# A hybrid recurrent layer on one core: convolutions, level sums, opening and decode-state matmuls rearranged

## The reference, cut to what matters

```python
proj = jnp.einsum('bld,de->ble', rmsnorm(x, g_mix_pre), w_in)     # 2048 -> 7 rounds of 1024 columns, and 16
# A: HGRN2, 4 heads, state 128x128, chunked recurrence with decays
att = jnp.einsum('bhtd,bhsd,bhtsd->bhts', qi, ki, dec)
o = jnp.einsum('bhts,bhse->bhte', att, vi) + jnp.einsum('bhtd,bhde->bhte', qi * jnp.exp(b), S)
# B: gated DeltaNet, 8 heads: width-4 causal convolution + SiLU on q, k, v, then
sol = triangular_solve(eye + A, rhs)
u = sol[..., :DV] - jnp.einsum('bhtd,bhde->bhte', sol[..., DV:], S)
S_new = jnp.exp(b_last) * S + jnp.einsum('bhsd,bhse->bhde', ki * jnp.exp(b_last - b), u)
# C: RG-LRU, 512 channels, behind a width-4 causal convolution, times a GELU gate
x = x + rmsnorm(concat([oa, ob, oc]) @ w_out, g_mix_post)
x = x + rmsnorm((silu(h2 @ w_gate) * (h2 @ w_up)) @ w_down, g_ffn_post)     # h2 = rmsnorm(x, g_ffn_pre)
```

## Time and profile before

| | |
|---|---|
| median of three runs | 1403.34 us |
| profiled execution, its own time | 1404.58 us |
| its span, first to last instruction | 1402.9 us |
| PE busy | 1380.7 us, 98% |
| DVE busy | 839.1 us, 60% |
| ACT busy | 688.8 us, 49% |
| PE's granted clock, mean | 0.995 of full speed |

### The profile page before, as it was taken

One profiled execution on the slowest core, in us unless ns is written; L12 is line 12 of the kernel. 1 busy time (PEld: TensorE's weight loads), 2 busy tenths in 40 slices (PEclk: granted clock), 3 DMA queues, 4 the chain that ended last, 5 costly groups with the idle time before them and its releaser, 6 DMA issues.

```text
span 1402.9 us, 27846 instructions
## 1 busy us (share of the span) xinstructions
PE 1380.7 (98%) x11299; PEld 1356.7 (97%) x11299; DVE 839.1 (60%) x1137; ACT 688.8 (49%) x960; POOL 74.6 (5%) x154
## 2 busy tenths in 40 slices
PE   8999999999999899999999999999999999999998
PEld 6999999999999899999999999999999999999998
DVE  6778686866596957566655555555555544444443
ACT  6545656565565665555444444444444433343333
POOL 4010101010201000200000000000000000000000
PEclk9999999999999999999999999999999999999999
DMA  6453636363556455544655555555555555555552
GB/s 222 135 172 100 198 92 199 106 186 109 174 154 179 121 154 179 186 134 153 211 180 180 181 179 183 180 181 180 183 181 182 180 181 181 180 180 180 181 180 77
DMA packets 225253, 234.07 MB, mean 167 GB/s; under 512 B 10443, under 2 KB 220526, under 8 KB 224900
## 3 DMA queue, kind: packets, MB, share of 16 engines
q1 hardware_dynamic: 220500, 218.86, 50.0%
q0 software_dynamic: 4672, 14.04, 3.6%
HBM read 223.45 MB, written 9.65 MB: 166 GB/s over the span
## 4 chain that ended last, share of the span: by engine, by line
PE 89%; DVE 6%; ACT 2%; issue 2%; DMA 1%; SPq 0%; DVEq 0%; ACTq 0%
PE ps L626 26%; PE ps L627 26%; PE ps L628 26%; PE ps L805 1%; PE ps L913 1%; DVE w_lo L1602 1%; PE ps L821 1%; DVE conv L1748 1%; DVE TT L1836 1%; ACT w_hi L1147 1%; DVE rs L1849 1%; DMA xtok<-in_x_prompt_dram 1%; PE ps L755 1%; PE ps L745 1%; PE ps L1096 0%
## 5 line engine op out<-in xcount | busy, mean ns | idle before, releaser
L1602 DVE TENSOR_TENSOR w_lo<-raw,w_hi 128x1024 fp32r<-128x1024 f32 x408 | 500.1, 1227 | 438.0 <-ACT w_hi L1147 436.2
L1147 ACT ACTIVATE w_hi<-raw 128x1024 fp32r<-128x1024 f32 x408 | 432.1, 1061 | 572.3 <-PE ps L628 570.9
L626 PE MATMUL ps<-act_hi,w_hi 128*128 128x264 f32 x2296 | 666.2, 290 | 0.3 <-DVE xT L1662 0.3
L627 PE MATMUL ps<-act_lo,w_hi 128*128 128x264 f32 x2296 | 653.1, 284 | 0.0
L628 PE MATMUL ps<-act_hi,w_lo 128*128 128x264 f32 x2296 | 652.2, 284 | 0.0
L627 PEld LDWEIGHTS ps<-act_lo,w_hi 128*128 128x128 f32 x2296 | 434.5, 189 | 1.5
L626 PEld LDWEIGHTS ps<-act_hi,w_hi 128*128 128x128 f32 x2296 | 434.2, 189 | 1.8 <-DVE xT L1662 0.4
L628 PEld LDWEIGHTS ps<-act_hi,w_lo 128*128 128x128 f32 x2296 | 433.1, 189 | 0.0
L627 PE MATMUL ps<-hid_lo,w_hi 128*128 128x264 f32 x696 | 197.9, 284 | 0.0
L626 PE MATMUL ps<-hid_hi,w_hi 128*128 128x264 f32 x696 | 197.7, 284 | 0.0
L628 PE MATMUL ps<-hid_hi,w_lo 128*128 128x264 f32 x696 | 197.6, 284 | 0.0
(11 more groups left out here) (365 smaller groups left out, 1125.5 us busy)
## 6 DMA issues: line engine op xcount, KB each, us to landing
raw<-in_w_in_dram SPq DMA_DIRECT2D x112, 512.0 KB, 3.6
raw<-in_w_gate_dram SPq DMA_DIRECT2D x88, 512.0 KB, 3.5
raw<-in_w_up_dram SPq DMA_DIRECT2D x88, 512.0 KB, 3.5
raw<-in_w_down_dram SPq DMA_DIRECT2D x88, 512.0 KB, 3.5
raw<-in_w_out_dram SPq DMA_DIRECT2D x32, 512.0 KB, 3.6
out_dram<-Ss POOLq DMA_DIRECT2D x12, 512.0 KB, 5.0
Ss<-in_state_gdn_dram POOLq DMA_DIRECT2D x8, 512.0 KB, 6.4
xtok<-in_x_prompt_dram SPq DMA_DIRECT2D x2, 1024.0 KB, 6.0
```

Source lines behind the costliest of these rows:

```text
L626: pe.matmul(out, wh, x_hi[:, kk], start=(kk == begin), stop=False)
L627: pe.matmul(out, wh, x_lo[:, kk], start=False, stop=False)
L1147: return act.activation(out, in_, f, **kw)
L1602: tt(w_lo[:, slot], raw[:, slot], w_hi[:, slot].bitcast(F32), sub).then_inc(lo_done, 1)
```

## The change

Six things are changed; nothing is taken out of the computation.

1. DeltaNet rounds: DVE writes k and q of each state into a block of 32 columns (`kq_st`, zero elsewhere). PE uses this block as the stationary operand and the state as the moving one, sixteen matmuls in half-chunks 8 and 9, each group of 32 output partitions of bank 7 taking every fourth of them. ACT copies the bank out at position 5, PE turns it back with four transposes at half-chunk 11, and DVE reads every 32nd column.
2. HGRN2 rounds: the same for q (`q_st`) and the outputs, in one block at half-chunk 23, the copy by ACT at position 12 and the transposes at half-chunk 25.
3. The sum over eight levels becomes three adds of 512, 256 and 128 columns.
4. `ln_exp_tables` in `a_step` is no longer called.
5. The group-C convolutions move from DVE's positions 4 and 8 to 12 and 14, and from ACT's 6 and 10 to 13 and 15.
6. In the opening `turn_input(1)` becomes four `keep_busy` matmuls, and the three turns stand behind halves 0, 2 and 4.

```diff
@@ PE, b_step
-                if 7 <= hp <= 10:
-
-                    if hp == 7:
+                if hp in (8, 9):
+
+                    if hp == 8:
...
-                    for x in range(4 * hp - 28, 4 * hp - 24):
-                        last = pe.matmul(ps[:, 7, 2 * x:2 * x + 2], Ss[:, x, :],
-                                         nrm[:, :, x // 8, L + x % 8], start=True, stop=True)
-                    if hp == 10:
-                        last.then_inc(mx["ks"], 1)
+                        pe.wait_ge(mx["kp"], 2 * n + 2)
+                    for x in range(8 * hp - 64, 8 * hp - 56):
+                        c = 32 * (x % 4)
+                        last = pe.matmul(ps[c:c + 32, 7, P * (x // 4):P * (x // 4) + P], kq_st[:, x, :], Ss[:, x, :],
+                                         start=True, stop=True)
+                    if hp == 9:
+                        last.then_inc(mx["kw"], 1)
...
                 if hp == 11:
+                    pe.wait_ge(mx["kc"], n + 1)
+                    for g in range(4):
+                        last = pe.transpose(ps[:, 7, g * P:g * P + P], XM[:, g, :], ident)
+                    last.then_inc(mx["ks"], 1)
@@ PE, a_step
-                if 24 <= hp <= 26:
...
+                if hp == 23:
+                    pe.wait_ge(mx["sn"], 4 * n + 4)
+                    pe.wait_ge(a_["qp"], 2 * k + 2)
+                    for x in range(16):
+                        c = 32 * (x % 4)
+                        last = pe.matmul(ps[c:c + 32, 7, P * (x // 4):P * (x // 4) + P], q_st[:, x, :], Ss[:, x, :],
+                                         start=True, stop=True)
+                    last.then_inc(a_["vw"], 1)
+                if hp == 25:
+                    pe.wait_ge(a_["vc"], k + 1)
+                    for g in range(4):
+                        last = pe.transpose(ps[:, 7, g * P:g * P + P], QK[:, g, :], ident)
+                    last.then_inc(a_["vs"], 1)
@@ PE, opening
-                if hp in (0, 2):
-                    turn_input(2 + hp // 2)
+                if hp in (0, 2, 4):
+                    turn_input(1 + hp // 2)
...
-            turn_input(1)
+            keep_busy(4, 0, 2)
@@ ACT
+                if pos == 5:
+                    act.wait_ge(mx["kw"], n + 1)
+                    A(XM, quad(7)).then_inc(mx["kc"], 1)
...
-                    ln_exp_tables()
...
                 if pos == 12:
+                    act.wait_ge(a_["vw"], k + 1)
+                    A(QK[:, :, :], quad(7)).then_inc(a_["vc"], 1)
...
-                    if kind == "c" and pos in (6, 10):
-                        free_qkv(r, q - 1)
-                        silu_conv(12 + q - 1, q - 1, ACT.Copy)
                     mixer(pos)
+                    if kind == "c" and pos in (13, 15):
+                        i = (pos - 13) // 2
+                        free_qkv(r, i)
+                        silu_conv(12 + i, i, ACT.Copy)
@@ DVE
                 if pos == 0:
...
+                    dve.memset(u[:, :, :], 0.0).then_inc(mx["kp"], 1)
...
                 if pos == 3:
+                    dve.wait_ge(mx["kp"], 2 * n + 1)
+                    dve.tensor_copy(kq_st[:, :, 0:2].rearrange("p (j b) m -> p j b m", j=2),
+                                    nrm[:, :, :, L:T].rearrange("p m j b -> p j b m")).then_inc(mx["kp"], 1)
...
+                if pos == 11:
+                    dve.memset(q_st[:, :, :], 0.0).then_inc(a_["qp"], 1)
+                    dve.wait_ge(a_["qp"], 2 * k + 1)
+                    dve.tensor_copy(q_st[:, :, 0], q_s).then_inc(a_["qp"], 1)
...
-                    dve.tensor_reduce(attT[:, x, :], prod.rearrange("p l t -> p t l"), AX.X, ALU.add)\
-                        .then_inc(a_["rd"], 1)
+                    tt(prod[:, 0:4], prod[:, 0:4], prod[:, 4:8], add).then_inc(a_["rs"], 1)
+                    dve.wait_ge(a_["rs"], 2 * c + 1)
+                    tt(prod[:, 0:2], prod[:, 0:2], prod[:, 2:4], add).then_inc(a_["rs"], 1)
+                    dve.wait_ge(a_["rs"], 2 * c + 2)
+                    tt(attT[:, x, :], prod[:, 0], prod[:, 1], add).then_inc(a_["rd"], 1)
...
-                    if kind == "c" and pos in (4, 8):
-                        chained[0] = CV * (q - 1)
-                        convolve(12 + q - 1, (q - 1) % 2, 12 * CV, params[:, C_BIAS + 2 * (q - 1):C_BIAS + 2 * q])
                     mixer(pos)
+                    if kind == "c" and pos in (12, 14):
+                        i = (pos - 12) // 2
+                        chained[0] = CV * i
+                        convolve(12 + i, i, 12 * CV, params[:, C_BIAS + 2 * i:C_BIAS + 2 * i + 2])
```

More of the change, by code:

```diff
@@ L158, in hybrid_layer @@
         TM = rsv[:, 512:1024].rearrange("p (x t) -> p x t", x=4)
+        kq_st = u[:, :, :].rearrange("p a (c i) -> p (a c) i", i=32)
         lev = put("lev", [P, LEVELS, 512], offset=place["decay"])
@@ L178, in hybrid_layer @@
                 put("umv_a", [P, 4, P], F32R, offset=place["hist_b"])]
+        q_st = put("q_st", [P, 16, 32], offset=place["hist_b"])
         ca = put("ca", [P, 4, T], offset=place["decay"])
@@ L291, in hybrid_layer @@
             "oc",
+            "kp",
+            "kw",
+            "kc",
             "ks",
@@ L333, in hybrid_layer @@
             "rd",
+            "rs",
+            "qp",
+            "vw",
+            "vc",
             "vs",
@@ L793, in b_step @@
                 if hp == 11:
+                    pe.wait_ge(mx["kc"], n + 1)
+                    for g in range(4):
+                        last = pe.transpose(ps[:, 7, g * P:g * P + P], XM[:, g, :], ident)
+                    last.then_inc(mx["ks"], 1)
                     pe.wait_ge(mx["qkp"], n + 1)
-                    pe.matmul(ps[:, 7, 32:48], ones[:, :], small[:, 0, :], start=True, stop=True).then_inc(mx["qk"], 1)
+                    pe.matmul(ps[:, 7, 2:18], ones[:, :], small[:, 0, :], start=True, stop=True).then_inc(mx["qk"], 1)
                 if 12 <= hp <= 23:
@@ L914, in a_step @@
                     last.then_inc(a_["at"], 1)
-                if 24 <= hp <= 26:
[L916 to L923, removed]
+                if hp == 23:
[11 more added lines that the diff above has]
+                    last.then_inc(a_["vs"], 1)
+                if hp == 24:
+                    pe.wait_ge(a_["pr"], 8 * k + 8)
                 if hp == 24:
@@ L1811, in b_step @@
                     dve.wait_ge(mx["qk"], n + 1)
-                    kq = ps[:, 7, 0:32].rearrange("p (x two) -> p x two", two=2)
+                    kq = ps[:, 7, :].rearrange("p (x i) -> p x i", i=32)
                     n5 = 6 * n
@@ L1815, in b_step @@
                     tt(small[:, 4, :], kq[:, :, 0], spair[:, 0, :], mul).then_inc(mx["us"], 1)
-                    dve.tensor_copy(small[:, 5, :], ps[:, 7, 32:48]).then_inc(mx["us"], 1)
+                    dve.tensor_copy(small[:, 5, :], ps[:, 7, 2:18]).then_inc(mx["us"], 1)
                     dve.wait_ge(mx["us"], n5 + 1)
@@ L1969, in a_step @@
                             .then_inc(a_["pr"], 1)
-                    dve.wait_ge(a_["pr"], 8 * k + 2 * x + 2)
-                    dve.tensor_reduce(attT[:, x, :], prod.rearrange("p l t -> p t l"), AX.X, ALU.add)\
-                        .then_inc(a_["rd"], 1)
+                    c = 4 * k + x
+                    dve.wait_ge(a_["pr"], 2 * c + 2)
+                    tt(prod[:, 0:4], prod[:, 0:4], prod[:, 4:8], add).then_inc(a_["rs"], 1)
[3 more added lines that the diff above has]
+                    tt(attT[:, x, :], prod[:, 0], prod[:, 1], add).then_inc(a_["rd"], 1)
                 if pos == 13:
@@ L1979, in a_step @@
                     dve.wait_ge(a_["vs"], k + 1)
-                    dve.tensor_copy(oT[:, :, L:T], ps[:, 7, 0:16].rearrange("p (j b) -> p j b", j=2))\
+                    dve.tensor_copy(oT[:, :, L:T], ps[:, 7, :].rearrange("p (j b i) -> p j b i", j=2, i=32)[:, :, :, 0])\
                         .then_inc(mx["os"], 1)
```

## The result

The changed kernel takes 1396.92 us (median of six runs, 1395.26 to 1397.27) against 1403.98 us for the kernel before (six runs beside them, 1401.23 to 1408.97): a ratio of 0.9945, 95% interval 0.9934 to 0.9957. The prediction was 1396.5 us. The profiled execution took 1397.27 us, its span is 1395.6 us, 7.3 less than before.

A forecast was written before the change was run, and what follows sets the result against it. PE's work, waits and clock bound the kernel. Opening +2.0, rounds 1 to 3 +3.4, round 4 -1.9, round 5 -3.3, round 6 -7.0: -6.8 on 1404.58, 1397.8; 1.24 lower as median, 1396.5 us (range 1390 to 1404.5).

The forecast's parts named there:

- Rounds 1 to 3, gain 0, two falls of the clock, +3.4: Half-chunk 14 waits for DVE, so PE's saving becomes idle; the clock falls in two of three rounds, +3.4 us (0 to 5.1).
- The block, 1.2 us and 0.44 for the transposes: Rounds 1 to 4: sixteen state matmuls take 1.2 instead of 3.5 us, four added transposes 0.44; PE's work falls 1.9.
- round 4, -1.9: Round 4, without convolutions: PE sets the pace, so its saved work shows, -1.9 us (bounds +0.4 and -2.3).
- Round 5, -3.3: Round 5: table load gone, wait 0.6 us shorter, half a clock fall saved, output block -1.9; -3.3 us (-0.2 to -4.7).
- Round 6, -7.0: Round 6: becomes like round 5 without its convolutions, -3.7, plus round 5's own -3.3; -7.0 us (-2 to -9).
- The part for the convolutions alone, -3.7: Round 6: convolutions leave DVE's row ahead of `umv_a`, their new place costs 0; 66.7 instead of 70.4 us, -3.7.
- Opening, +2.0: Opening: chunk 3's weights come late, PE waits 1.5 us, gate columns start at 37.5 instead of 35.34; +2.0 us (-0.5 to +3.7).
- No fall of the clock: Rival, half-chunk 14 of rounds 1 to 3: the longer idle leaves the clock up; -10.2 us, 1393.1, chance 0.22.
- Tiles one after another: Rival, state and output blocks: tiles do not run side by side, the operand change does nothing; -3.3 us, 1400.0, chance 0.13.
- A longer slow stretch at half-chunk 14: Rival, rounds 1 to 3: clock down 6.8 us each, opening and last rounds slowed too; +3.3 us, 1406.6, chance 0.12.
- The level sums: Round 5: three adds replace one reduce on DVE, which had 1.83 us of idle just ahead; effect 0.

## Why the prediction was right, point by point

- **Rounds 1 to 3, gain 0, two falls of the clock, +3.4.** Right: 0, +1.6 and +1.6, +3.2. The idle was 2.1 us and not 2.4, because the new block costs more than the 1.2 us (next point). That DVE's row sets half-chunk 14 is shown from two sides: work added to PE there costs nothing (two dummies), work taken from DVE's row gives 1.8 us a round and saves the falls. That the clock fell in two of the three rounds was a choice between two cases, and luck as to the number: with the same waits of 1.9 to 2.1 us it fell in one round with the opening put back and in three with the table load put back. Nor does a wait of 1.3 us keep the clock up each time, as I took from one row: in two of the twelve traces a slow stretch follows the wait of 1.3 us ahead of the FFN.
- **The block, 1.2 us and 0.44 for the transposes; round 4, -1.9.** The mechanism was right, the block mis-sized by 0.2: 179.20 - 176.99 - 1.46 = 0.75 and 182.81 - 179.20 - 2 x 1.46 = 0.69 us, 1.4 in all; the transposes took 0.44. That makes 3.5 - 1.4 - 0.44 = 1.7, which is also what PE's wait in rounds 1 to 3 grew by (1.6). Round 4 gained 0.4 more than that, 2.1: half-chunk 13, where PE had stood for ACT's copy, went from 2.79 to 2.35 us; why it did was not tried. One column position shows the parallel part.
- **Round 5, -3.3.** The mechanism was right, the size 1.0 short: -4.3. The wait shrank by 0.46 (2.13 to 1.67) and half-chunk 13 by 0.29, 0.75 for the table load instead of 0.6; the new output block gave 1.9 as said (from the last L910 to the first L939 12.05 us before, from L926 to L961, the same two lines, 10.14 after; not tried alone); the fall of the clock, of which I took half, did not come in this execution. The level products, PE's wait in it and the new block:

```profile
408.03 0.49 PE L926 MATMUL ps<-u,nrm 128*128 128x128 f32 x2 [1.67 <-DVE lev L1990]
...
426.02 1.08 PE L936 MATMUL ps<-Ss,q_st 128*32 128x128 f32 x32
```

- **Round 6, -7.0.** -6.3 (-3.7, round 5's -4.3, and +1.7 because there the clock did fall, 0.97 in the round's row). The convolutions' new place cost nothing: everything behind the round is 889.1 us as against 889.0. The part for the convolutions alone, -3.7, is shown by itself.
- **Opening, +2.0.** The chain (last turn, four activations, `w_lo`, copies, gate columns) came out to the tenth: the wait 1.54 for 1.5, the gate columns at 37.48 for 37.5 (37.5 - 35.34 is 2.2, so the +2.0 was rounded down). Yet the term was mis-sized: I set it against an opening in which the clock was down, as if that belonged to it. Without that the step costs 3.5 us. The change looked cheaper there only because the profiled execution of the kernel before had a slow stretch.
- **Rivals.** No fall of the clock: refuted in the profile after, though it happens in single rounds. Tiles one after another: refuted. A longer slow stretch at half-chunk 14: it was 3.4 us, not 6.8, and behind the three turns and the wait in the opening the clock did not fall (1.00 from 14 to 48 us).
- **The sum.** That it came within 0.4 us of the median is in part luck: round 5 gained 1.0 more and round 6 0.7 less than forecast, both mostly by where the clock happened to fall, and the two falls in rounds 1 to 3 were a guess.
- **The level sums** (taken as 0) were not tried alone.

## What to carry to other kernels

Before work is taken from an engine, find the next wait behind it and ask what row of the other engine ends there; if that row starts ahead of the saved work and has no gap, the saving becomes idle time, and on TensorE idle time of two microseconds cost a slow stretch on top in six of nine rounds here, 1.6 us each. Then look into that row for instructions that need not stand there: moving four of DVE's gave 10 us in the changed kernel. Most of that is what the new matmuls had saved and could not show: without the move they gave nothing in rounds 1 to 3, and without them the move would have met waits of 0.3 to 0.5 us only (not tried). And when a step is set against the trace of one execution, look whether a slow stretch in that trace belongs to the step or to the execution.

## What the runs showed of the hardware that I had not expected

The same idle is not always followed by a slow clock. PE's wait of 1.9 to 2.1 us at half-chunk 14 was followed by a row of 0.98 in rounds 2 and 3 of the changed kernel, in round 2 alone with the opening put back, and in all three rounds with the table load put back. The wait of 1.7 us in round 5 was followed by a slow stretch in none of eight traces, that of 1.8 us in round 6 in three of the same eight (the changed kernel, the opening put back, two dummies). A shorter wait does not rule it out: all twelve traces have a wait of 1.3 us ahead of the FFN's first matmuls, and in two of them (the convolutions of round 6 moved alone, the dummy in rounds 5 and 6) the clock fell about 2 us after it. Two openings with the same instructions on PE differed in the same way (0.51 in the earlier trace rows, 1.00 with the opening put back). What decides it from one execution to the next stays open.

What is clear is the other side: in the nine traces in which PE's wait at half-chunk 14 is 0.51 us or less, whether by the old states, by dummies, by one column position or by the moved convolution, no round 1 to 3 has a slow stretch. A fall cost 1.4 to 1.7 us in the opening and in the rounds, so part of the spread between runs of one kernel, 1.3 to 7.7 us, can come from it.

Four 32-column tiles at four positions ran at three times the speed of one position over sixteen records (0.64 against 1.93 us).
